# Sample rows' output projection as fp32 column quadrants among the prompt tiles

## The reference

```python
x = x + concat(attention(z), gmlp(z)) @ w_out        # z = rmsnorm(x) @ w_in, both kinds of rows
t = rmsnorm(x)                                       # * norm_ffn_g
g_logits = t @ w_rg + b_rg;  g_idx = argmax(g_logits)          # 4 groups
e_logits = t @ w_re + b_re;  top 2 of the 8 experts in group g_idx, softmax weights
for e in range(32):
    y += combine[:, e] * ((silu(t @ w_gate[e]) * (t @ w_up[e])) @ w_down[e])
out = rmsnorm(x + y) * final_norm_g
```

## Time and profile before

| | |
|---|---|
| runs of the kernel before | 731.46, 731.99, 733.0 us; median 731.99 |
| profiled execution | 733.94 us, span 732.2 us |
| mean granted PE clock | 0.995 of full speed |
| busy, PE | 705.8 us, 96% of the span |
| busy, PE weight loads | 554.9 us, 76% |
| busy, DVE | 563.1 us, 77% |
| busy, ACT | 452.1 us, 62% |
| busy, POOL | 144.3 us, 20% |
| DMA | 178.78 MB, mean 244 GB/s |

### The profile page before, as it was taken

How to read it: one execution, slowest core, us unless ns; L and a number is a source line. 1 busy time by engine, 2 the same in 40 slices (tenths; PEclk the granted TensorE clock), 3 DMA queues, 4 the chain that set the end, 5 groups by cost and what they waited for, 6 DMA issues and landing times. The chain is left out here.

```text
span 732.2 us, 11990 instructions
## 1 busy us (share of the span) xinstructions
PE 705.8 (96%) x3839; PEld 554.9 (76%) x3839; DVE 563.1 (77%) x871; ACT 452.1 (62%) x708; POOL 144.3 (20%) x154
## 2 busy tenths in 40 slices
PE   6899999999999999999998999999999999999995
PEld 3587887887778778788787788888888888888841
DVE  4865866866868885363885999999999999999857
ACT  6554354453455642221323988988888888888745
POOL 1110110110110111000013133333333333331114
PEclk9999999999999999999999999999999999999999
DMA  8991930330311637314249999999999999998758
GB/s 337 282 299 57 212 86 0 86 86 0 86 59 65 233 122 292 115 49 162 98 171 352 373 369 365 393 395 380 390 391 395 381 392 386 366 411 332 260 200 340
DMA packets 79642, 178.78 MB, mean 244 GB/s; under 512 B 41184, under 2 KB 45224, under 8 KB 71416
## 3 DMA queue, kind: packets, MB, share of 16 engines
q1 hardware_dynamic: 70104, 160.80, 61.0%
q0 software_dynamic: 9216, 16.93, 6.1%
q10 hardware_dynamic: 288, 0.62, 0.3%
HBM read 159.58 MB, written 35.37 MB: 266 GB/s over the span
## 5 line engine op out<-in xcount | busy, mean ns | idle before, releaser
L2162 DVE TENSOR_TENSOR wg_lo<-wg,wg_hi 128x1024 fp32r<-128x1024 f32 x128 | 150.5, 1216 | 3.0 <-ACT wg_hi L1360 2.9
L1360 ACT ACTIVATE wg_hi<-wg 128x1024 fp32r<-128x1024 f32 x128 | 128.8, 1062 | 5.4 <-PE psZ L1224 2.7
L1224 PE MATMUL psZ<-wg_hi,xg_hi 128*128 128x512 f32 x256 | 103.2, 403 | 0.6 <-ACT xg_hi L1360 0.6
L1224 PE MATMUL psZ<-wg_hi,xg_lo 128*128 128x512 f32 x256 | 101.1, 395 | 0.0
L1224 PE MATMUL psZ<-wg_lo,xg_hi 128*128 128x512 f32 x256 | 100.6, 393 | 0.0
L831 PE MATMUL psZ<-wi_hi,xT_hi 128*128 128x512 f32 (+1 forms) x256 | 96.9, 378 | 1.8 <-DVE wi_lo L1757 1.8
L831 PE MATMUL psZ<-wi_hi,xT_lo 128*128 128x512 f32 (+1 forms) x256 | 94.0, 367 | 0.0
L831 PE MATMUL psZ<-wi_lo,xT_hi 128*128 128x512 f32 (+1 forms) x256 | 94.0, 367 | 0.0
L2316 DVE TENSOR_TENSOR wd_lo<-wd,wd_hi 128x2048 fp32r<-128x2048 f32 x31 | 71.0, 2292 | 22.4 <-ACT wd_hi L1360 22.4
L2497 POOL DMA_INDIRECT y_d<-y_t,idx_dst x32 | 46.8, 1462 | 192.0 <-ACT y_t L1360 192.0
L2493 POOL DMA_INDIRECT xg<-h_d,idx_src x32 | 57.8, 1805 | 28.3 <-issue 15.8
(11 more groups left out here) (328 smaller groups left out, 1305.7 us busy)
## 6 DMA issues: line engine op xcount, KB each, us to landing
wg<-w_gate SPq DMA_DIRECT2D x32, 1024.0 KB
wg<-w_up SPq DMA_DIRECT2D x32, 1024.0 KB
wd<-w_down SPq DMA_DIRECT2D x32, 1024.0 KB
y_d<-wo_stage SPq DMA_DIRECT2D x1, 4608.0 KB
mix_d<-mix_t SPq DMA_DIRECT2D x9, 512.0 KB, 3.2
m_t<-mix_d SPq DMA_DIRECT2D x9, 512.0 KB, 3.7
h_d<-h_t SPq DMA_DIRECT2D x9, 512.0 KB, 3.9
wi_raw<-w_in SPq DMA_DIRECT2D x4, 1024.0 KB, 14.9
```

Of the source, the lines that this page charges most:

```text
L1224: last = nc.tensor.matmul(psZ[z][:], a[:, c, :], w, start=(n == 0), stop=(n == 3 * DC - 1))
L1360: return nc.scalar.activation(out, in_, ACT.Copy)
L2162: tt(wg_lo[k][:, :, c, :], wg[k][:, :, c, :], wg_hi[p][:].bitcast(F32), ALU.subtract).then_inc(s_wgl, 1)
```

## The change

The sample rows leave tile 8. Their projection is now `sample_proj(n)`, n = 0 to 3: for two chunks each, four fp32 matmuls of 8 rows by 256 columns, each into its own quarter of the partitions of one bank (rows 0, 32, 64, 96), without splitting. The weights come from `w_out` anew, unsplit, two chunks at a time into two buffers `wq` (`load_wq`), each pair after the block before it has read the buffers. Blocks stand in (5,1) after 4 chunks, behind tile 4's `route` at the end of tile 5, in (6,0) after 7 chunks, in (6,1) after 4 chunks. ACT copies the four quarters to `oq_t`, SP stores them to `zo_d` in DRAM and loads them back as 8 rows `zo_t`, POOL adds x and multiplies by the gain, ACT scales and stores.

The attention of the sample rows moves ahead for this: weights into (4,1) after 4 chunks, values into (5,0). The clearing of `mix_t` goes. Tile 7 is now the last: its h_t comes by ACT and its transposes in two parts (`t_h_low` within (7,1), `t_h_high` behind it), and half (7,1) also holds tile 6's `route` and `route_sum` and the sample rows' transposes and router. T_A is 5, so that 4 tiles (5, 6, 7, 8) are ranked at the end; the experts of the first five are chosen earlier in DVE's tile 6, and the splitting of expert 0's first pieces moves from tile 6 to tile 5 (`T_PRE`). Of expert 1, the down weights load before the last half ends; gate and up stay behind it, and the `h_d` store follows them.

```diff
-T_A = T - 3
+T_A = T - 4
+T_PRE = T_P - 3
...
+            def load_wq(n):
+                for c in (2 * n, 2 * n + 1):
+                    if c < QPK:
+                        for k in range(NKV):
+                            sp.dma_start(wq[c % 2][k * HD:(k + 1) * HD], wo_att[k][:, c, :]).then_inc(s_wo[0], 16)
+                    else:
+                        sp.dma_start(wq[c % 2][:], wo_r[:, c, :]).then_inc(s_wo[0], 16)
...
-                if 0 < t < T_P:
+                if 0 < t < T_P - 1:
                     sp.wait_ge(s_op, 2 * t)
                     sp.wait_ge(s_mix, 16 * (t + 2))
                     load_m(t + 1)
...
+                if t == T_P - 2:
+                    sp.wait_ge(s_pj, 2)
+                    load_wq(2)
                 if t > 0:
                     store_h(t - 1)
+                if t == T_P - 3:
+                    sp.wait_ge(s_pj, 1)
+                    load_wq(1)
...
                     load_expert(0)
-                elif t == 6:
-                    sp.dma_start(rows(mix_d, T_P), mix_t[:]).then_inc(s_mix, 16)
-
-            for t in range(T):
+                    sp.wait_ge(s_u, T)
+                    load_wq(0)
+                elif t == T_P - 2:
+                    sp.wait_ge(s_pj, 3)
+                    load_wq(3)
+                    sp.wait_ge(s_pj, 4)
+                    sp.dma_start(x1b[0:N_SAMPLE], rows(x_rows, T_P, N_SAMPLE)).then_inc(s_xs, 16)
+                    sp.wait_ge(s_oq, 1)
+                    for j in range(4):
+                        sp.dma_start(zo_d[:, 256 * j:256 * (j + 1)], oq_t[32 * j:32 * j + N_SAMPLE, :]).then_inc(s_zy, 16)
+                    load_down(0, 1, 1, s_wd[1])
+                    sp.wait_ge(s_op, 2 * T_P - 2)
+                    sp.wait_ge(s_zy, 16 * 13)
+                    sp.dma_start(zo_t[:], zo_d).then_inc(s_xs, 16)
+
+            for t in range(T_P):
                 stage2(t)
 
-            sp.wait_ge(s_op, 2 * T)
-            load_expert(1)
-            store_h(T_P)
+            sp.wait_ge(s_oq, 2)
+            sp.dma_start(rows(h_d, T_P, N_SAMPLE), hs_t[:]).then_inc(s_zy, 16)
+            sp.wait_ge(s_op, 2 * T_P)
+            load_gate_up(0, 1, 1, s_wg[1])
+            store_h(T_P - 1)
...
+            def sample_proj(n):
+
+                if n == 0:
+                    pe.wait_ge(s_sv, 10)
+                pe.wait_ge(s_wo[0], 16 * (WO_PARTS[0] + (4, 8, 10, 12)[n]))
+                for c in (2 * n, 2 * n + 1):
+                    for j in range(4):
+                        last = nc.tensor.matmul(psS[32 * j:32 * j + N_SAMPLE, 512:768], mix_t[:, c * P:c * P + N_SAMPLE],
+                                                wq[c % 2][:, 256 * j:256 * (j + 1)], start=(c == 0), stop=(c == DC - 1),
+                                                skip_group_check=True)
+                last.then_inc(s_pj, 1)
...
+                elif (t, h) == (4, 1):
+                    out_chunks(t, h, range(0, 4))
+                    sample_weights()
+                    out_chunks(t, h, range(4, DC)).then_inc(s_op, 1)
+                elif (t, h) == (5, 0):
                     out_chunks(t, h, range(0, 2))
-                    out_chunks(t, h, range(2, 5))
+                    for c in range(DC):
+                        if c >= 2:
+                            last = out_chunks(t, h, (c,))
+                        sample_values(c)
+                    last.then_inc(s_op, 1)
+                elif (t, h) == (5, 1):
+                    out_chunks(t, h, range(0, 4))
+                    sample_proj(0)
+                    out_chunks(t, h, range(4, DC)).then_inc(s_op, 1)
+                elif (t, h) == (6, 0):
+                    out_chunks(t, h, range(0, 2))
+                    route_sum(t - 2)
+                    out_chunks(t, h, range(2, 7))
+                    sample_proj(2)
+                    out_chunks(t, h, range(7, DC)).then_inc(s_op, 1)
+                elif (t, h) == (6, 1):
+                    out_chunks(t, h, range(0, 4))
+                    sample_proj(3)
+                    out_chunks(t, h, range(4, DC)).then_inc(s_op, 1)
+                elif (t, h) == (T_P - 1, 1):
+                    out_chunks(t, h, range(0, 2))
+                    route(t - 1)
+                    out_chunks(t, h, range(2, 4))
+                    route_sum(t - 1)
+                    t_h_sample()
+                    out_chunks(t, h, range(4, 6))
+                    t_h_low()
+                    route_sample()
+                    out_chunks(t, h, range(6, DC)).then_inc(s_op, 1)
...
-                elif (t, h) in ((3, 1), (5, 1)):
-                    for c in range(DC):
-                        last = out_chunks(t, h, (c,))
-                        (sample_scores if t == 3 else sample_values)(c)
...
+            def t_h_low():
+
+                pe.wait_ge(s_x1, 2 * T_P - 1)
+                pe.wait_ge(s_hTa, T_P - 1)
+                pe.wait_ge(s_hTv, T_P - 1)
+                transposes(lambda j: x1(T_P - 1)[:, j * P:(j + 1) * P], 4, psT[1]).then_inc(s_hTp, 1)
+
+            def t_h_high():
+
+                pe.wait_ge(s_x1, 2 * T_P)
+                pe.wait_ge(s_lgo, 2 * T_P - 1)
+                transposes(lambda j: x1(T_P - 1)[:, (4 + j) * P:(5 + j) * P], 2, psT[0])
+                pe.wait_ge(s_hTa, T_P)
+                transposes(lambda j: x1(T_P - 1)[:, (6 + j) * P:(7 + j) * P], 2, psT[1]).then_inc(s_hTp, 1)
...
+                    if t == 5:
+                        sample_out()
                     t_h(t - 1)
                 out_half(t, 1)
-                if t == 5:
-                    sample_out()
                 if t == 1:
                     pv(T_P - 1, 1)
                     t_h(0)
-                elif t == T_P:
-                    route(t - 1, range(0, DC // 2))
-                    t_h_sample()
-                    route(t - 1, range(DC // 2, DC))
-                    route_sample()
+                elif t == T_P - 1:
+                    route(t, range(0, DC // 2))
+                    t_h_high()
+                    route(t, range(DC // 2, DC))
                 else:
                     route(t - 1)
                 if t == 3:
                     sample_rows()
-                elif t == 4:
-                    sample_weights()
+                elif t == 5:
+                    sample_proj(1)
+                elif t == 6:
+                    pe.wait_ge(s_rv, 1)
+                    ranks(psS, 0, T_A).then_inc(s_rp, 1)
+                    counts(psO, 0, T_A, True, T - T_A + 1)
...
+            def proj_out():
+
+                act.wait_ge(s_pj, 4)
+                for j in range(4):
+                    last = copy(oq_t[32 * j:32 * j + N_SAMPLE, :], psS[32 * j:32 * j + N_SAMPLE, 512:768])
+                last.then_inc(s_oq, 1)
...
             def stage2(t):
-                if t < T_P:
+                if t < T_P - 1:
                     m_hi(t + 1)
+                if t == T_P - 2:
+                    choice_first(0, T_A, 0)
...
-                elif t == T_P - 1:
-                    choice_exps(0, T_A, 0)
-                if t < T_P:
+                elif t == T_P - 2:
+                    choice_second(0, T_A, 0)
+                    proj_out()
+                if t < T_P - 1:
                     square2(t)
                 else:
+                    square_sample()
                     square_half(0)
+                    h_sample()
+                    h_low()
                     square_half(1)
-                if t == T_A:
+                    h_high()
+                if t == T_PRE:
...
-                dve.wait_ge(s_mix, 16 * T_P)
-                step(nc.vector.memset(mix_t[:], 0.0))
...
+            def gain_mult(k):
+
+                dve.wait_ge(s_x1, 2 * T_P - 1 + k)
+                if k == 1:
+                    dve.wait_ge(s_oq, 1)
                 d = slice(512 * k, 512 * (k + 1))
-                last = tt(psS[:, d], x1(T_P)[:, d], ffg[:, d], ALU.mult)
+                last = tt(psS[:, d], x1(T_P - 1)[:, d], ffg[:, d], ALU.mult)
                 if k == 1:
...
             def stage2(t):
-                last = t == T_P
-                early = t == T_P - 1
-                if t < T_P:
+                last = t == T_P - 1
+                early = t == T_P - 2
+                if not last:
                     m_lo(t + 1)
                 if t > 2:
                     logits_out(t - 2)
                 if early:
                     dve.wait_ge(s_lgo, 2 * T_A)
                     choose_group(0, T_A)
+                    choose_experts(0, T_A)
+                    cp(tr_bf[:], cst[:, C_TR:C_TR + P])
+                    nc.vector.memset(on_bf[:], 1.0).then_inc(s_rv, 1)
...
-                    elif t == 5:
-                        sample_weights_out()
...
+                elif t == 5:
+                    sample_values_out()
+                    sample_rows_out()
                 if last:
-                    sample_mult(0)
+                    gain_mult(0)
```

(49 more changed lines are left out.)

100 lines of the change are left out of this document (65 added, 35 removed).

## The result

The changed kernel takes 737.46 us (median of 8 executions, 734.0 to 739.19) against 732.42 for the kernel before (731.46 to 734.07): ratio 1.0065, interval 1.0052 to 1.0079. It is slower by 5.0 us. The forecast was 2.9 faster, with 725.2 to 733.4 as its range.

A forecast was written before the change was run, and what follows sets the result against it. PE, busy 96% of the span, was taken as the bound, with the stretch from its last projection matmul to the first expert. −13.9 + 6.5 + 5.0 − 0.5 = −2.9 against the median 731.99 gave 729.1 us, range 725.2 to 733.4.

The forecast's parts named there:

- Removed, −13.9: Tile 8's two halves leave PE's projection: 8.35 + 5.57 = 13.9 us saved.
- Added PE work, +6.5: Before the last projection matmul: four blocks 4.3, ranks 0.6, sample transposes 0.6, `t_h_low` 0.4, `route_sample` 0.6; together 6.5 us.
- Waits, +5.0: New PE waits at five places before the last projection matmul, taken as additive: sum 5.0 us.
- second pair of `wq`: PE waits 1.4 us for this load at the end of tile 5; bounds 0.7 and 3.7 or more.
- `lgT`: Tile 6's `route_sum` in (7,1) waits 1.4 us for this input, behind DVE's one-hots, `residual` and `gain_mult`.
- `selp`: In (4,1) PE waits 1.5 us for this DVE input of the sample weights; bounds 1.0 and 2.5.
- rival E: The clock falls to half in two or three stretches of 2.0 us during PE gaps: 731.5 us, chance 0.08.
- Behind E, −0.5: From E (PE's last projection matmul) to the first expert: gather begins +0.2 later, takes 0.7 less; sum −0.5 us.
- Rival F: The tail gives nothing, or the change does less, the gather bound by its own latency: 730.4 us, chance 0.05.
- B (waits absorbed): Loads land as PE comes and `lgT` is ready, so 3.2 of the 5.0 go: 725.9 us, chance 0.17.
- C (half-partition loads): 64-partition loads are slow, landing in 7.5, so the second pair's wait adds 3.6: 732.7 us, chance 0.12.
- D: Sample rows come back late through DRAM and PE waits 4.9 us in (7,1): 734.0 us, chance 0.10.

The follow-up runs named there:

- e_sel: Changed kernel with the second `wq` pair loaded early, `lgT` evicted ahead of the one-hots, and sample weights two chunks later in (4,1): 728.0 us, ratio 0.9944.
- a_fill1: Changed kernel with twelve filler matmuls on PE ahead of the wait for the second `wq` pair: 734.92 us, ratio 1.0041.
- a_fill2: Changed kernel with filler matmuls in both gaps, twelve ahead of the `wq` wait and eight ahead of the `lgT` wait: 734.53 us, ratio 1.0032.
- a_lg: Changed kernel with the eviction of `lgT` moved ahead of the one-hots and two 512-column operations on DVE in tile 7: 732.68 us, ratio 1.0006.
- a_two: Changed kernel with the `wq` bytes in two half-partition loads of 512 KB instead of four of 256 KB: 736.54 us, ratio 1.0057.
- a_again: The changed kernel run once more, unaltered, for its second profile: 737.0 us, ratio 1.0064.
- e_down: Changed kernel with second `wq` pair early and `lgT` ahead of the one-hots, expert 1's down weights loaded behind the last half again: 727.51 us, ratio 0.9932.
- a_port: Changed kernel with POOL's multiply of the sample rows delayed until `lgT` is evicted: 734.46 us, ratio 1.0027.

## Why the prediction was wrong

**Removed, −13.9: right.** Tile 8 is gone. Tile 6's `route_sum`, which stood in it, is now in tile 7 and counts below.

**Added PE work, +6.5: too small.** In e_sel the stretch has no wait and full clock, so what it holds beyond 64.35 − 13.9 = 50.4 is the added work: 58.6 − 50.4 = 8.2. The blocks cost 0.98 each, 3.9 in all, and with the other pieces of the forecast 6.2, so these were not too small. Missed were tile 6's `route_sum`, 0.4, which had been counted as gone with tile 8, and the seams, 1.4: the 168 matmuls of the projection in this stretch take 41.8 from start to start in e_sel, and 40.4 in the kernel before without tile 8. Pieces stand between them in 22 places instead of 17. The first matmul behind a piece stands some 0.32 ahead of the next, and the last one ahead of a block or a router 0.32 to 0.44; the others 0.23.

**Waits, +5.0: two were mis-sized.** The second pair of `wq` cost 3.0 instead of 1.4: the landing of whole-tile loads was taken for a half-partition load. `lgT` cost 2.1 instead of 1.4: DVE was held up by POOL's multiply, which the forecast had costed at nothing as work on a free POOL. `selp` cost 1.1 (1.5), the fourth pair 0.4 (0.7, where its own 4.9 against 4.3 are 0.6), the third 0 (0), though 0.5 to 1.0 in a_fill1, a_fill2 and a_lg. Sum 6.6.

**The clock, 0: this is the step that failed.** The forecast named it as rival E with 2.4 us and a chance of 0.08, and argued from the 1.8 us wait of the earlier trace rows, behind which the clock stayed up. That row says nothing of a gap of 3, which lay within the sum's own bounds for the second pair. A stretch costs some 1.6 us (table: 1.6 left after, 3.1 for two in the second profile). The clock's own rows say the same: 0.74, 0.50 and 0.91 in the three rows from 340 on are (0.26 + 0.50 + 0.09) × 2 = 1.7 us of PE's work. The wait for `lgT` led to a stretch in the second profile, at 2.2 us, and to none in the first, at 2.1; in a_two 2.3 led to none and in a_fill1 2.2 to one. So the length alone doesn't decide it, and what does isn't shown. That executions differ by it can account for the 5 us between this kernel's: half clock over some stretch costs half its length and lowers the mean by that share of the span, so a thousandth of mean clock is an estimated 0.7 us of a span of 734, and the six long executions of the first measurement, 0.003 to 0.007 lower than the fastest, took 2.0 to 5.2 us more. The six of a_again do not show it.

**Behind E, −0.5: nothing.** `idx_src` ended 13.3 us after E (13.1 forecast), the gather began at 14.7 (14.0) and took 3.75 (4.0). That the chain goes over `idx_src` was right; what the gather won was lost ahead of it. Rival F was right in that the tail gave nothing, and the early down load gives nothing either (e_down).

So in the first profile: −13.92 + 8.17 + 6.55 + 1.59 = +2.39 to E. Two of these terms were taken as remainders, so that it adds up proves nothing; what carries it is that the table's column is near zero wherever the clock stayed up. The second profile shows +4.2. The median's 5.0 needs the second stretch in most executions and some 1 us more, which no profile shows and which stays open.

From −2.9 to +5.0 are 7.9 us: 1.7 of work, 1.6 of waits, 0.5 behind E, 3.1 of clock with two stretches, and that 1. Without the clock the forecast would have been 729.1 + 1.7 + 1.6 + 0.5 = 732.9: no faster than the kernel before, but within its range. The clock is the largest term, and it was put at nothing.

**The rivals.** B (waits absorbed) did not happen in the changed kernel; the versions that win, at 727.6, are without the waits because edits took them out. C (half-partition loads) was right in kind: +1.6 of the +3.6 given. D did not happen: PE waits for neither `zo_t` nor POOL in any profile. In the first, POOL's add began 4.5 us after the issue of `zo_t` (4.9 forecast) and ended at 365.6, and PE came at 372.4. E happened, next to C: with what they cost, +1.6 and +3.1, they make 4.7 of the 7.9 us. The chances had treated them as exclusive, though the longest waits are those behind which the clock always fell.

## What to carry to other kernels

A wait on an otherwise full TensorE can cost more than its length: removing 2.1 us of it gave 4.3 here, and 3.4 gave 4.3, so look at the granted clock behind every gap of 2 us and more, and take more than one profile, since executions differ. Before a small load feeds a full engine, find a row for the same number of partitions, not only for the same bytes; and when work moves onto an idle GpSimd, or in its order there, look at what VectorE does with two SBUF inputs beside it.

## What the runs showed of the hardware

- Loads onto 64 partitions: 1 MB in 6.9 us as four and 7.2 as two, beside other loads, with the DMA engines fully busy at 227 to 253 GB/s; 1 MB as two loads onto 128 partitions in 4.8, and 366 GB/s at the same busy share.
- Ahead of E the granted clock fell to 0.50 behind waits of 3.0 to 3.2 us in five of five profiles, behind 2.1 to 2.5 in three of five, behind 1.8 and less in none. It stayed down for 3 to 7 us. Behind E, in the routing, it fell in every profile, behind two waits of 1.4 to 1.9 with some 0.3 us of matmuls between them. Fillers of 128x128 matmuls, 0.24 us each, kept it up.
- A VectorE operation with two SBUF inputs, 0.31 alone, took 0.68 to 1.60 us beside a GpSimd operation of 2.38 us, and ended 0.2 after it; the one-hots, 1.55 alone, took 3.73 beside it. A GpSimd operation of 0.18 took 1.79 beside that operation and the one-hots (a_port).
- Eight fp32 matmuls of 8x256 into four partition quarters take 1.0 us.
